# Six gate projections as seven half-size products each, and the neighbourhood query projection moved ahead

## The chip, the cores and the metric

One core of one Trainium2 chip runs the whole kernel in one launch. The metric is the device time of that launch in microseconds. All data are 32-bit floats.

## The reference, cut to what matters

One layer of a hybrid backbone for 256 latent tokens with 256 context tokens, 1024 wide. The normalised and modulated tokens `h` go through one wide input projection. Its parts feed a neighbourhood attention (nq, nk, nv), a gated scan in two directions (hq, ff, fb, hi, hg), a grouped-query attention (gq, gkv), and three gates of 1024 columns. Then the branches are merged and a mixture of 16 experts follows:

```python
zl = split_in(h_lat @ w_in)
zc = split_in(h_ctx @ w_in)
...
y_lat = branch_merge((a_lat, b_lat, c_lat), zl[11:14], w_branch, w_out)
...
def branch_merge(branches, gate_logits, w_branch, w_out):
    y = 0
    for i in range(N_BRANCHES):
        y = y + jax.nn.sigmoid(gate_logits[i]) * (branches[i] @ w_branch[i])
    return y @ w_out
```

The gates (`zl[11:14]`) are needed for the 256 latent tokens only; hi, nk and nv are needed for latent and context tokens alike.

## The kernel before

Five engines work side by side, each through an instruction list of its own, joined by semaphores. The order of each list is written out by hand; nothing is scheduled by a planner. TensorE (`pe`) multiplies, VectorE (`dve`) and ScalarE (`act`) empty its banks, GpSimd (`pool`) does side work, SyncE (`sp`) issues the transfers one after the other. A wait of any engine holds all that stands behind it in its list.

**Weights.** `FRONT` (line 43) lists the projections in the order of loading. Each takes a slot of 2 MB, three slots in turn (`SLOT_OF`); the load of a projection waits until the one three places ahead of it is multiplied (SP's loop, lines 486 to 527). Behind the loads of hq, hg, hi, nk, nq and nv, SP issues four each of 32 parts of the ada weights (`PARTS_BEHIND`, line 113), each as soon as GpSimd has used the part two before it (line 519); two more stand behind gq and six behind gate0. On the way to gate5 SP loads the first expert units, and one more (`load_unit(LAP - 3)`, line 499) when all pooled sums are done; `x_nat` is loaded behind gate2 (line 527).

**GpSimd's list.** After four sums of `hT` it goes through the parts q = 0 to 31 (line 620): a part of two 512-wide slices is multiplied by the conditioning (line 644 in one product of 1024 elements, or for q = 11 to 19 line 642 in two scalings of 512), and added into a running sum (lines 647 to 650). Between parts stand the operand sums for the projections that are computed in seven products: `weight_sums` (three sums of 128 x 1024, lines 606 to 609) and `last_weight_sum` (one, line 616), for hi before q = 9 and 12, for nk before q = 14 and 16, for nv before q = 20 and 24. Then come the rotary steps of the grouped-query attention (lines 660 to 678), ended by `gqa_ready`.

**Seven products.** hi, nk and nv (`SEVEN`, line 72) are 1024 x 512 weights times 1024 x 512 tokens. Each is cut in half in all three dimensions and computed as seven half-size products (`part_product`, line 937; 16 matmul records of 256 columns and 128 x 128 weights each, two records for one 32-bit matmul) in place of eight. Product 1 is copied out by ScalarE (`copy_first`), seven adds of VectorE (`add_product`, line 1671) combine them. Products 5 to 7 need operand sums of GpSimd, and product 3 needs the last one.

**The level stretch of TensorE** (lines 1195 to 1232). After the fills (`fill`, line 887) of ff, fb, hq, hg come eight levels of the scan, `level(0)` to `level(7)`. Each needs VectorE's `join` and ScalarE's `level_keys` of the level before. Between two levels lie two products of hi or nk. Behind level 7 stand both nq fills with the context state (`ctx_state`, line 1043) between them, then `across` (line 1022), the products of nv and the outputs.

**The attention loop** (line 1237) has 16 steps of eight heads and two tiles, neighbourhood attention first, then grouped-query. A step of TensorE is: scores (line 1113), in steps 0 to 5 one turn of a pooled sum, values of the step before (line 1136), one fill of gq, gkv or a gate, transposes of the normalised probabilities (line 1121). VectorE takes maxima, normalises (two scalings of 512, line 1791) and copies the transposes (line 1619); ScalarE takes exponentials. With steps 3 and 4 VectorE also squares and norms the grouped queries (line 1762). The 12 gate fills (line 908, 32 records of 256 columns) lie in steps 4 to 15; ScalarE copies them out. In step 7 the grouped queries and keys are turned, which needs `gqa_ready`. Behind the loop the branch projections br0 to br2 (line 925) begin at once.

## Time and profile before

| | us |
|---|---|
| median of 3 runs | 698.49 (697.67 to 698.77) |
| profiled execution | 697.12 |
| its span in the trace | 695.1 |
| TensorE busy (granted clock 0.997 on average) | 679.4 |
| VectorE, ScalarE, GpSimd busy | 325.3, 106.7, 239.1 |
| front stage up to the first products of hi | 0 to 116 |
| level stretch, up to the last product of nv | 116 to 231 |
| attention loop | 232 to 400 |
| branches, output projection, router | 400 to 483 |
| experts and end | 483 to 695 |

In the trace, a line names an engine, the line of the kernel, the operation, what it writes and reads, and a count. The busy time of TensorE is the union of its matmuls; they overlap in the pipeline, so that one lasts longer than it adds to a run of many. "Idle before" names the time an engine stood still ahead of a group, and what released it.

### The profile page before, as it was taken

To read this page: it belongs to the slowest core of one execution; us is meant where nothing else is said; L and a number is where in the kernel's file an instruction comes from. 1 tells how busy PE (TensorE), PEld (TensorE's weight loads), DVE (VectorE), ACT (ScalarE), POOL (GpSimd) and SP (SyncE) were. 2 spreads that over 40 slices of the span, in tenths; PEclk is the share of its full clock that TensorE was granted. 3 is DMA by queue.
4 is the path that set the end of the run, shared out by engine and by line. 5 is a ranking of instruction groups with operands and counts; after the bars stand their busy time and mean duration, and the time that the engine had idled before them with its cause. 6 is when DMAs were issued, how large, how long until landed. Compare 5 with 4: busy or idle time off the path is not lost.

```text
span 695.1 us, 8395 instructions
## 1 busy us (share of the span) xinstructions
PE 679.4 (98%) x3432; PEld 445.6 (64%) x3432; DVE 325.3 (47%) x531; ACT 106.7 (15%) x188; POOL 239.1 (34%) x155
## 2 busy tenths in 40 slices
PE   9999999999999999999999999999999999999995
PEld 5444587979989567777877888667435534434431
DVE  3459697796632687754343233336303203202214
ACT  4011011111001222321221140013000000000013
POOL 0029999999999594800000000000000000000014
PEclk9999999999999999999999999999999999999998
DMA  8993551341417744433491149866999999999993
GB/s 353 416 407 101 211 227 74 140 180 61 185 59 270 305 128 172 186 122 121 180 410 60 78 134 424 350 256 237 397 417 423 418 422 421 420 421 421 421 414 132
DMA packets 29512, 183.74 MB, mean 264 GB/s; under 512 B 3543, under 2 KB 5975, under 8 KB 14624
## 3 DMA queue, kind: packets, MB, share of 16 engines
q1 hardware_dynamic: 27456, 178.72, 64.7%
q0 software_dynamic: 1584, 3.97, 1.5%
q8 instruction: 29, 0.48, 0.3%
q10 hardware_dynamic: 432, 0.49, 0.2%
q14 instruction: 11, 0.09, 0.0%
HBM read 178.15 MB, written 6.82 MB: 266 GB/s over the span
## 4 chain that ended last, share of the span: by engine, by line
PE 75%; POOL 15%; DMA 4%; DVE 3%; issue 2%; ACT 1%; SPq 0%; POOLq 0%; DVEq 0%
PE bank L1431 21%; PE bank L908 14%; PE bank L944 6%; PE bank L925 6%; PE bank L1389 4%; POOL sb L644 3%; PE bank L931 3%; PE bank L1190 3%; PE bank L1113 2%; POOL sb L650 2%; PE bank L1136 2%; POOL sb L649 2%; PE bank L912 2%; PE bank L1121 2%; POOL sb L642 2%
## 5 line engine op out<-in xcount | busy, mean ns | idle before, releaser
L1431 PE MATMUL bank<-sb 128*64 128x512 f32 x768 | 166.8, 594 | 0.7 <-ACT sb L837 0.7
L685 POOL DMA_INDIRECT y_rows<-sb,token_rows x7 | 7.0, 1002 | 359.9 <-DVE sb L2049 335.1
L908 PE MATMUL bank<-sb 128*128 128x256 f32 x576 | 128.1, 381 | 0.0
L1431 PEld LDWEIGHTS bank<-sb 128*64 128x64 f32 x768 | 54.3, 137 | 106.5 <-issue 103.7
L908 PEld LDWEIGHTS bank<-sb 128*128 128x128 f32 x576 | 108.4, 190 | 16.2 <-issue 2.4
L944 PE MATMUL bank<-sb 128*128 128x256 f32 x336 | 74.1, 380 | 1.6 <-POOL sb L609 1.6
L944 PEld LDWEIGHTS bank<-sb 128*128 128x128 f32 x336 | 63.3, 190 | 9.9 <-POOL sb L609 1.8
L1619 DVE COPY sb<-bank 128x512 f32<-128x512 f32 x45 | 29.2, 684 | 82.5 <-PE bank L1121 54.4
L2009 DVE TENSOR_TENSOR sb<-sb,bank 128x512 f32<-128x512 f32 x8 | 5.5, 688 | 99.0 <-PE bank L1431 99.0
L644 POOL TENSOR_TENSOR sb<-sb 128x1024 f32<-128x1024 f32 x23 | 47.8, 2076 | 9.5 <-DMA sb<-ada_w 7.7
L925 PE MATMUL bank<-sb 128*128 128x256 f32 x192 | 41.9, 380 | 0.0
L925 PEld LDWEIGHTS bank<-sb 128*128 128x128 f32 x192 | 36.4, 190 | 5.0 <-issue 0.2
L650 POOL TENSOR_TENSOR sb<-sb 128x512 f32<-128x512 f32 x24 | 34.8, 1449 | 1.9
L642 POOL TENSOR_SCALAR sb<-sb 128x512 f32<-128x512 f32 x18 | 34.8, 1944 | 0.6
L649 POOL TENSOR_TENSOR sb<-sb 128x512 f32<-128x512 f32 x24 | 32.0, 1332 | 1.9
L2000 DVE TENSOR_SCALAR sb<-bank,sb 128x128 f32<-128x128 f32 x64 | 21.8, 404 | 17.8 <-PE bank L1389 17.6
L1190 PE MATMUL bank<-sb 128*128 128x512 f32 x64 | 29.0, 599 | 0.7 <-DVE sb L1571 0.7
L1389 PE MATMUL bank<-sb 128*128 128x128 f32 x224 | 27.9, 278 | 0.0
L904 PE MATMUL bank<-sb 128*128 128x512 f32 x64 | 27.6, 592 | 0.0
L792 ACT ACTIVATE sb<-bank,sb 128x512 f32<-128x512 f32 x32 | 21.8, 685 | 37.1 <-DVE sb L1784 37.1
L1389 PEld LDWEIGHTS bank<-sb 128*128 128x128 f32 x224 | 26.1, 192 | 0.0
L2049 DVE SCALAR_TENSOR_TENSOR sb<-bank,sb 128x512 f32<-128x512 f32 x14 | 10.5, 751 | 26.9 <-PE bank L1431 26.9
(260 smaller groups left out, 810.8 us busy)
## 6 DMA issues: line engine op xcount, KB each, us to landing
sb<-expert_w SPq DMA_DIRECT2D x90, 1024.0 KB, 17.6
sb<-front_w SPq DMA_DIRECT2D x19, 2048.0 KB, 8.4
sb<-ada_w SPq DMA_DIRECT2D x32, 512.0 KB, 3.7
sb<-ada_mix SPq DMA_DIRECT2D x4, 2048.0 KB, 19.8
sb<-expert_w SPq DMA_DIRECT2D x12, 512.0 KB, 10.9
sb<-xcT SPq DMA_DIRECT2D x4, 512.0 KB, 6.4
sb<-front_w SPq DMA_DIRECT2D x4, 512.0 KB, 20.5
y_rows<-sb SPq DMA_DIRECT2D x4, 512.0 KB, 24.0
```

Source lines behind the costliest of these rows:

```text
L642: last = pool.tensor_scalar(w[:, k, :], w[:, k, :], cvec[:, k0 + k, 0:1], None, ALU.mult)
L644: last = pool.tensor_tensor(w, w, cvec[:, k0:k0 + PART_K, 0:1].broadcast_to([P, PART_K, 512]), ALU.mult)
L649: link(pool.tensor_tensor(w[:, 0, :], w[:, 0, :], w[:, 1, :], ALU.add))
L650: ins = pool.tensor_tensor(ada_sum[g], ada_sum[g], w[:, 0, :], ALU.add)
L904: ins = pe.matmul(ps[:, :], lhs(w, k, i * P), hT[:, k, :], start=(k == 0), stop=(k == KD - 1))
L908: ins = pe.matmul(ps[:, c * L:(c + 1) * L], lhs(w, k, (2 * i + c) * P), hT[:, k, 0:L], start=(k == 0), stop=(k == KD - 1))
L925: ins = pe.matmul(ps[:, c * L:(c + 1) * L], lhs(w, k, (2 * i + c) * P, D), src[:, k, :], start=(k == 0), stop=(k == 3))
L944: ins = pe.matmul(o, left, right, start=(k == 0), stop=(k == 3))
L1190: ins = pe.matmul(banks[BANK_OF[i]][:, :], lhs(slot[0], k, i * P), hT[:, k, :], start=(k == 0), stop=(k == KD - 1))
L1389: ins = pe.matmul(banks[i][:, c * P:(c + 1) * P], x_nat[:, t, (4 * i + c) * P:(4 * i + c + 1) * P], S[:, t, :], start=(t == 0), stop=(t == ...
L1431: ins = pe.matmul(bank[e * CAP:(e + 1) * CAP, :], lhsT[:, k, e * CAP:(e + 1) * CAP], weights_at(k, e), start=(k == 0), stop=(k == parts - 1))
L1619: dve.tensor_copy(dst, shared_wait(n)[:, :]).then_inc(shared_out, 1)
```

## The change

Six things are changed. (1) The gates join `SEVEN`: each is cut in half in rows and columns of the weights and in tokens, so that its seven products are 128 columns wide (56 matmuls, 112 records). Products 2, 4 and 1 (`gate_first_half`) and 6, 7, 5 and 3 (`gate_second_half`) take the places of the two fills. GpSimd adds four sums per gate and four half-width sums of `hT` before q = 28; ScalarE copies product 1, VectorE adds seven products per gate. (2) nq is loaded ahead of hi, and its fills stand behind levels 0 and 1; the products of hi and nk move back by two levels, and the context state stands among those of nk. (3) GpSimd's sums for hi, nk and nv stand before later parts (13 and 16, 18 and 21, 24 and 26), and the two-scaling form is used from q = 5. (4) The sums of gate0 stand ahead of the rotary steps and those of the others behind them. (5) br0 waits until the last gate is summed. (6) `x_nat` and the expert unit LAP - 3 are loaded behind br2's weights. The diff, without bookkeeping of semaphore numbers, the renaming of waits and the rewritten `add_product`:

```diff
 ROUTES = GCOLS + NE
-FRONT = ["ff", "fb", "hq", "hg", "hi", "nk", "nq", "nv", "gq", "gkv"]
+FRONT = ["ff", "fb", "hq", "hg", "nq", "hi", "nk", "nv", "gq", "gkv"]
 FRONT += [f"gate{i}" for i in range(6)]
...
 WARM = (7, 4, 1, 3)
-BANK_OF = [{("ff", 3): 7, ("nq", 0): 0, ("nq", 1): 2}.get(f[:2], n % PBANKS) for n, f in enumerate(FILLS)]
+BANK_OF = [7 if f[:2] == ("ff", 3) else n % PBANKS for n, f in enumerate(FILLS)]
 ROW_GROUPS = (4, 5, 10, 11)
...
 PART_K = KD // PARTS
-PARTS_BEHIND = {name: range(4 * i, 4 * i + 4) for i, name in enumerate(("hq", "hg", "hi", "nk", "nq", "nv"))}
+PARTS_BEHIND = {name: range(4 * i, 4 * i + 4) for i, name in enumerate(("hq", "hg", "nq", "hi", "nk", "nv"))}
 PARTS_BEHIND["gq"], PARTS_BEHIND["gate0"] = range(24, 26), range(26, 32)
...
 STEPS = len(UNITS)
-FILLER = [n for n in range(fill_no("gq"), fill_no("br0"))]
+FILLER = [n for n in range(fill_no("gq"), fill_no("gate0"))]
 FILLER_AT = {i: [] for i in range(STEPS)}
 for _i, _n in enumerate(FILLER):
-    FILLER_AT[_i * STEPS // len(FILLER)].append(_n)
+    FILLER_AT[_i].append(_n)
 G_STEP = [i for i in range(STEPS) if fill_no("gkv", 1) in FILLER_AT[i]][0]
-GATE_FILLS = fill_no("gate5", 1)
+GATE_FILLS = fill_no("gate5")
+def gate_at(i):
+    return GATES[(i - len(FILLER)) // 2], (i - len(FILLER)) % 2
...
         w_sums = {"hi": [at(A0 + 1024 * i, 4, L) for i in range(2)]}
+        x_half_sums = [at(F0 + 8192 + 2048 + 512 * i, 4, P) for i in range(4)]
         w_sums["nk"] = w_sums["nv"] = [at(F0 + 2048 + 1024 * i, 4, L) for i in range(2)]
...
         spare = keep(NT * D, NT, D)
+        for g in GATES:
+            w_sums[g] = [spare[:, i, :].rearrange("p (k f) -> p k f", f=256) for i in range(2)]
         xT = [[at(C0 + 6144, 4, P), at(C0 + 6656, 4, P)],
...
         def out_part(name, fh, th):
+            if name in GATES:
+                c = 4 * GATES.index(name) + 2 * fh
+                return gates[:, c:c + 2, P * th:P * th + P]
             if name == "nk":
...
             return (v_hg if name == "hi" else na_v)[:, 2 * th:2 * th + 2, 256 * fh:256 * fh + 256]
-        def product_bank(name, m):
-            if m in part_bank:
-                return part_bank[m]
-            return banks[(m == 4) != (name != "hi")]
+        def x_half(kh, th):
+            return hT[:, 4 * kh:4 * kh + 4, P * th:P * th + P]
+        def product_out(name, m):
+            if name in GATES:
+                b, h = {1: (0, 0), 5: (0, 1), 3: (0, 0), 2: (1, 0), 4: (1, 1), 6: (2, 0), 7: (2, 1)}[m]
+                ps = banks[b][:, L * h:L * h + L]
+            else:
+                ps = (part_bank[m] if m in part_bank else banks[(m == 4) != (name != "hi")])[:, :]
+            return ps.rearrange("p (a b) -> p a b", a=2)
         def ada_place(g):
...
                     load_unit(8)
-                    sp.wait_ge(ada_summed, len(POOLED))
-                    load_unit(LAP - 3)
                 if name == "out0":
...
                     sp.dma_start(row5.rearrange("p (a b) -> p a b", a=2), d["b_rows"][:, 2:4, :]).then_inc(row5_in, 16)
+                if name == "br2":
                     sp.dma_start(x_nat, d["x_nat"]).then_inc(xnat_in, 16)
+                    load_unit(LAP - 3)
             sp.wait_ge(out_by["dve"], 4)
...
                     pool.wait_ge(fill_ready, multiplied("nk"))
+                if name in GATES[1:]:
+                    pool.wait_ge(part_ready, product_no(SEVEN[SEVEN.index(name) - 1], 5))
                 pool.tensor_tensor(s[0], w_part(name, 1, 0), w_part(name, 1, 1), ALU.add).then_inc(sums_ready, 1)
...
             def last_weight_sum(name):
-                pool.wait_ge(part_ready, product_no(name, 3))
+                pool.wait_ge(part_ready, product_no(name, 2))
                 pool.wait_ge(sums_ready, operand_no(name, 3))
...
             for q in range(PARTS * len(POOLED)):
-                if q == 9:
+                if q == 13:
                     weight_sums("hi")
-                if q == 12:
+                if q == 16:
                     last_weight_sum("hi")
-                if q == 14:
+                if q == 18:
                     weight_sums("nk")
-                if q == 16:
+                if q == 21:
                     last_weight_sum("nk")
-                if q == 20:
+                if q == 24:
                     weight_sums("nv")
-                if q == 24:
+                if q == 26:
                     last_weight_sum("nv")
+                if q == 28:
+                    pool.wait_ge(shared_out, shared_no("o", 1) + 1)
+                    link(pool.tensor_tensor(x_half_sums[0], x_half(0, 1), x_half(0, 0), ALU.subtract))
+                    link(pool.tensor_tensor(x_half_sums[1], x_half(1, 1), x_half_sums[0], ALU.subtract))
+                    pool.tensor_tensor(x_half_sums[2], x_half(1, 0), x_half_sums[1], ALU.subtract)
+                    pool.tensor_tensor(x_half_sums[3], x_half(1, 1), x_half(0, 1), ALU.subtract).then_inc(sums_ready, 1)
                 g, k0 = POOLED[q // PARTS], q % PARTS * PART_K
...
                 w = ada_part[q % 2].rearrange("p (k c) -> p k c", k=PART_K)
-                if 11 <= q < 20:
+                if 5 <= q < 20:
                     for k in range(PART_K):
...
                     pool.sem_inc(ada_summed, 1)
+            weight_sums(GATES[0])
+            last_weight_sum(GATES[0])
             pool.wait_ge(g_tab, 1)
...
             pool.tensor_tensor(kx, kx, gk, ALU.mult).then_inc(gqa_ready, 1)
+            for name in GATES[1:]:
+                weight_sums(name)
+                last_weight_sum(name)
             pool.wait_ge(rows_cleared, 16 * 2 * NT)
...
                     fill(n)
+                if i >= len(FILLER) and gate_at(i)[1] == 0:
+                    copy_first(gate_at(i)[0])
                 if i == G_STEP:
...
                     act.activation(g_ms, g_ms, ACT.Sqrt, bias=sm("eps"), scale=1.0 / HD).then_inc(rooted, 1)
-            act.wait_ge(out_by["act"], emptied(GATE_FILLS)[1])
+            act.wait_ge(out_by["sums"], emptied(GATE_FILLS)[1])
             for b in range(3):
...
                     wait_emptied(pe, before[-1])
-                if name == "nq":
-                    pe.wait_ge(out_by["sums"], sums_no("nk", 4))
                 if name == "gq":
                     wait_emptied(pe, fill_no("nv"))
+                if (name, i) == ("br0", 0):
+                    wait_emptied(pe, GATE_FILLS)
                 g = FRONT.index(name)
...
+            def gate_first_half(name):
+                g = GATES.index(name)
+                take_slot(FRONT.index(name))
+                if g == 0:
+                    wait_emptied(pe, fill_no("gkv", 1))
+                else:
+                    pe.wait_ge(out_by["sums"], sums_no(name, 0) - 3)
+                part_product(name, 2, w_part(name, 0, 1), x_half(1, 0))
+                pe.wait_ge(sums_ready, operand_no(name, 0))
+                part_product(name, 4, w_part(name, 1, 1), x_half_sums[2])
+                pe.wait_ge(out_by["sums"], sums_no(name, 0))
+                part_product(name, 1, w_part(name, 0, 0), x_half(0, 0))
+            def gate_second_half(name):
+                pe.wait_ge(sums_ready, operand_no(name, 2))
+                part_product(name, 6, w_sums[name][1], x_half_sums[1])
+                pe.wait_ge(sums_ready, operand_no(name, 3))
+                part_product(name, 7, w_part(name, 1, 0), x_half_sums[3])
+                pe.wait_ge(part_copied, SEVEN.index(name) + 1)
+                part_product(name, 5, w_sums[name][0], x_half_sums[0])
+                pe.wait_ge(sums_ready, operand_no(name, 4))
+                part_product(name, 3, w_part(name, 0, 1), x_half(1, 1))
             def take_shared(n):
...
             level(0)
+            fill(fill_no("nq", 0))
+            level(1)
+            fill(fill_no("nq", 1))
+            level(2)
             first("hi")
             fourth("hi")
-            level(1)
+            level(3)
             second("hi")
             sixth("hi")
-            level(2)
+            level(4)
             seventh("hi")
             fifth("hi")
-            level(3)
+            level(5)
             third("hi")
             first("nk")
-            level(4)
+            level(6)
             fourth("nk")
             second("nk")
-            level(5)
+            level(7)
             sixth("nk")
             seventh("nk")
-            level(6)
+            ctx_state()
             fifth("nk")
             third("nk")
-            level(7)
-            fill(fill_no("nq", 0))
-            ctx_state()
-            fill(fill_no("nq", 1))
             across()
...
                     fill(n)
+                if i >= len(FILLER):
+                    name, half = gate_at(i)
+                    (gate_first_half, gate_second_half)[half](name)
                 if i == GQA_TURN:
...
                 join(v)
-                if v == 2:
+                if v == 4:
                     sums_of_first("hi")
                     sums_of_seventh("hi")
-                if v == 3:
+                if v == 5:
                     sums_of_fifth("hi")
                     sum_of_third("hi")
-                if v == 5:
-                    sums_of_first("nk")
-                if v == 6:
-                    sums_of_seventh("nk")
-                    sums_of_fifth("nk")
-                if v == LEVELS - 1:
-                    sum_of_third("nk")
+            sums_of_first("nk")
+            sums_of_seventh("nk")
             for q in range(2):
                 shared_copy(shared_no("s0", q), S0[:, 4 * q:4 * q + 4, :].rearrange("p a b -> p (a b)"))
+            sums_of_fifth("nk")
+            sum_of_third("nk")
             for dr in range(2):
...
                     add_ada(g)
+                if i >= len(FILLER) and gate_at(i)[1] == 1:
+                    sums_of_first(gate_at(i)[0])
+                    sums_of_seventh(gate_at(i)[0])
                 if i == GQA_TURN:
...
                     shared_copy(shared_no("pT", 2 * i + e), probsT[:, e, :])
+                if i >= len(FILLER) and gate_at(i)[1] == 1:
+                    sums_of_fifth(gate_at(i)[0])
+                    sum_of_third(gate_at(i)[0])
                 if i == G_STEP:
```

## Rows read from the trace of the kernel before

**Rows 1.** The page: busy us; GB/s in 40 slices of 17.4 us

```profile
PE 679.4 (98%) x3432; PEld 445.6 (64%) x3432; DVE 325.3 (47%) x531; ACT 106.7 (15%) x188; POOL 239.1 (34%) x155
...
GB/s 353 416 407 101 211 227 74 140 180 61 185 59 270 305 128 172 186 122 121 180 410 60 78 134 424 350 256 237 397 417 423 418 422 421 420 421 421 421 414 132
```

**Rows 2.** Groups of instructions by line: busy us, mean ns of one, idle

```profile
L644 POOL TENSOR_TENSOR sb<-sb 128x1024 f32<-128x1024 f32 x23 | 47.8, 2076 | 9.5 <-DMA sb<-ada_w 7.7 <-POOL sb L650 0.5
...
L642 POOL TENSOR_SCALAR sb<-sb 128x512 f32<-128x512 f32 x18 | 34.8, 1944 | 0.6
...
L1389 PE MATMUL bank<-sb 128*128 128x128 f32 x224 | 27.9, 278 | 0.0
...
L1680 DVE TENSOR_TENSOR sb<-bank,sb 128x512 f32<-128x512 f32 x21 | 14.5, 689 | 9.9 <-PE bank L944 8.7
```

**Rows 3.** TensorE's timeline, level stretch: start, us, line, count, idle

```profile
154.05 7.15 PE L944 MATMUL bank<-sb 128*128 128x256 f32 x32 [1.62 <-POOL sb L609]
...
171.51 7.07 PE L944 MATMUL bank<-sb 128*128 128x256 f32 x32
178.42 1.95 PE L1011 MATMUL bank<-sb 128*128 128x128 f32 x16
180.21 7.07 PE L908 MATMUL bank<-sb 128*128 128x256 f32 x32
187.12 3.73 PE L1043 MATMUL bank<-sb 128*128 128x128 f32 x32
...
197.60 1.95 PE L1022 MATMUL bank<-sb 128*128 128x128 f32 x16
```

**Rows 4.** GpSimd in order of time, parts and operand sums

```profile
80.18 1.89 POOL L644 TENSOR_TENSOR sb<-sb 128x1024 f32<-128x1024 f32 x1
...
168.26 2.35 POOL L616 TENSOR_TENSOR sb<-sb 128x1024 f32<-128x1024 f32 x1 [0.24 <-POOL sb L650]
170.59 3.10 POOL L642 TENSOR_SCALAR sb<-sb 128x512 f32<-128x512 f32 x2
...
195.75 2.35 POOL L606 TENSOR_TENSOR sb<-sb 128x1024 f32<-128x1024 f32 x1 [0.24 <-POOL sb L650]
...
203.78 2.88 POOL L644 TENSOR_TENSOR sb<-sb 128x1024 f32<-128x1024 f32 x1
...
208.09 1.90 POOL L644 TENSOR_TENSOR sb<-sb 128x1024 f32<-128x1024 f32 x1
...
280.32 1.90 POOL L662 TENSOR_TENSOR sb<-sb 128x1024 f32<-128x1024 f32 x1 [11.44 <-DVE sb L1770]
```

**Rows 5.** TensorE in order of time, loop steps 4 and 15

```profile
277.88 7.17 PE L908 MATMUL bank<-sb 128*128 128x256 f32 x32
284.89 1.20 PE L1121 MATMUL bank<-sb 128*128 128x128 f32 x8
...
398.90 1.04 PE L1121 MATMUL bank<-sb 128*128 128x128 f32 x8
399.77 3.62 PE L925 MATMUL bank<-sb 128*128 128x256 f32 x16
```

**Rows 6.** VectorE in order of time, in the attention loop

```profile
256.94 3.06 DVE L1791 TENSOR_SCALAR sb<-sb 128x512 f32<-128x512 f32 x2
...
283.35 1.37 DVE L1791 TENSOR_SCALAR sb<-sb 128x512 f32<-128x512 f32 x2
...
329.00 1.29 DVE L1619 COPY sb<-bank 128x512 f32<-128x512 f32 x2 [4.75 <-PE bank L1121]
...
332.83 0.88 DVE L1791 TENSOR_SCALAR sb<-sb 128x512 f32<-128x512 f32 x2
339.08 1.29 DVE L1619 COPY sb<-bank 128x512 f32<-128x512 f32 x2 [5.38 <-PE bank L1121]
```

**Rows 7.** Busy time by stretch: each engine, PEclk, DMA share, GB/s

```profile
686.00:695.00 9.00, 1.61 (x4) 0.38 (x2) 3.88 (x7) 4.57 (x13) 2.52 (x3) 0.79 0.33 120
```

**Rows 8.** TensorE in order of time, its first work

```profile
1.33 5.16 PE L1164 MATMUL bank<-sb 128*128 128x256 f32 x14 [1.33 <-DVE sb L1532]
```

More of the change, by code:

```diff
@@ L66, in earlier, with product_no @@
     return [m for m in range(n) if SLOT_OF[m] == SLOT_OF[n]]
-SEVEN = ("hi", "nk", "nv")
+GATES = tuple(f"gate{i}" for i in range(6))
+SEVEN = ("hi", "nk", "nv") + GATES
 PRODUCTS = 6
-def product_no(name, last):
-    return PRODUCTS * SEVEN.index(name) + last
+def product_no(name, m):
+    return PRODUCTS * SEVEN.index(name) + ((2, 4, 1, 6, 7, 5) if name in GATES else (1, 4, 2, 6, 7, 5)).index(m) + 1
 def sums_no(name, last):
@@ L86, in operand_no @@
 def operand_no(name, last):
-    return 1 + 4 * SEVEN.index(name) + last
+    return 1 + (name in GATES) + 4 * SEVEN.index(name) + last
 def group_fills(name):
@@ L744, in fill @@
                     act.activation(gkv[:, 2 * i:2 * i + 2, :], two, ACT.Copy).then_inc(done, 1)
-                elif name[:4] == "gate":
-                    c = 4 * int(name[4:]) + 2 * i
-                    if c == 0:
-                        act.wait_ge(shared_out, shared_no("s0", 1) + 1)
-                    act.activation(gates[:, c:c + 2, :], two, ACT.Copy).then_inc(done, 1)
             def level_keys(v):
@@ L762, in copy_first @@
                     act.wait_ge(silu_hg, 2)
-                act.activation(out_part(name, 0, 0), product_bank(name, 1)[:, :].rearrange("p (a b) -> p a b", a=2),
-                               ACT.Copy).then_inc(part_copied, 1)
-            for n in range(fill_no("hi")):
+                act.activation(out_part(name, 0, 0), product_out(name, 1), ACT.Copy).then_inc(part_copied, 1)
+            for n in range(fill_no("nq")):
                 fill(n)
```

45 lines of the change are left out of this document (22 added, 23 removed).

## Prediction

> **What bounds the kernel now.** First the busy shares: TensorE is busy for 98% of the span, VectorE 47%, GpSimd 34% [rows 1]. So any TensorE time that is removed comes off the end, unless something else becomes late. Then TensorE's order of time in the level stretch [rows 3]: the reader is to see one stream without holes except 1.62 us in front of a product, and its releaser, the GpSimd line L609. So GpSimd is nearly late there already. Its own timeline [rows 4] shows it working without a pause from 80 to 222 us: it is the second engine of this stage, and its 34% is an average over a span in whose second half it idles. Last the attention loop: TensorE has its 7.0 us fill in every step and the softmax chain of VectorE and ScalarE lies beside it [rows 5, 6].
>
> **The change part by part.**
>
> *Gate products.* How far apart do records follow each other? A run of 32 with 256 columns lasts 7.07 us and the next line starts 6.91 after its start, so 0.216 us each; a run of 32 with 128 columns, each with a weight block of its own, lasts 3.73 us, of which the last record's length is 0.278: (3.73 - 0.278) / 31 = 0.111 us [rows 2, 3]. A gate is now two fills of 32 records; one takes 7.01 us from its start to that of the transposes behind it (277.88 to 284.89) [rows 5], 0.1 more than 32 x 0.216. After: 7 products x 8 matmuls x 2 records = 112 records x 0.111 = 12.5, plus twice 0.1, 12.7 us against 14.0. Six gates: -8.0 us, all on TensorE, which sets the end. Range of the pitch: 0.111 to 0.1245 (the group of L1389 over its count, 27.9/224) [rows 2], so between -8.0 and +0.5. I take 0.111, as the row is a like stream.
>
> The Trainium skill ("TensorE: Matmul & The Clock Gate", "Back-to-back issue gap") speaks against this edit: it says that in a stream of weight load and matmul pairs the spacing is set by both, and gives 81 ns where the columns alone would take 56. By its ratio 1.45 the 112 records would take about 18.1 us and the gates would get slower, by some 24 us in all. The trace disagrees: half the columns come at 52% of the pitch [rows 3].
>
> *GpSimd's queue before attention.* This is the costly part. `last_weight_sum("nk")` stood before part q = 16 of the pooled ada sums; it now stands before q = 21, and TensorE's product 3 of nk waits for it. GpSimd is a serial queue: it ends that sum at 168.26 + 2.35 = 170.6 us now [rows 4]. Ahead of it come q = 16 to 19 (170.59 to about 195.5, 24.9 us), q = 20 (203.78 to 208.09, 4.3, of which 1.0 is contention that will then lie later: 3.3) [rows 4], and six parts q = 5 to 10 change from one 1.89 us product to two scalings of together 3.10 us [rows 4], 1.2 each, 7.2 in all. Sum 170.6 + 24.9 + 3.3 + 7.2 = 206.0 us. When will TensorE want it? Third product of nk now starts at 171.51 + 3.53 = 175.0. Ahead of it are now put level 7 (1.8), both nq fills (6.9 each) and the context state (3.6) [rows 3]: 19.2 us, and the 1.6 us wait goes: 192.6. So TensorE waits 13.4 us there, and `across` starts at 206.0 + 3.45 = 209.4 instead of 197.60 [rows 3]: +11.8 us. An earlier wait, on the last sum of hi, is paid within this one. Bounds: the conversion may cost up to 1.8 us a part (twice the mean of L642 less that of L644) [rows 2], +3.6; or less contention of VectorE in 97 to 112 us and in the levels may give up to 6 back. So +6 to +16.
>
> Moving nq ahead costs TensorE nothing in itself: same records, its weights simply take the turn of hi's. The weights of hi now follow parts 8 to 11 in SP's queue, so they are asked for when q = 9 is done, about 113 us, and are wanted at 134 by TensorE and about 131 by GpSimd; cover of some 9 us after a load. The nv sums: GpSimd from 206 takes q = 21 to 23 (14 us) and three sums of 2.35 (the first at 195.75 now) [rows 4], more if VectorE contends, to about 229; TensorE wants the third of them 11.8 us later than now, at about 232. Cover 3 us, cost nothing; if it is gone, the same amount late.
>
> *Clock.* TensorE would stand still for over 8 us, which it does nowhere between its first and last work now. The only such row: at the end, TensorE stops at 687.6 and the mean granted clock of 686 to 695 is 0.79 [rows 7], thus the lower level, 1.2 GHz, for about 3.8 us. And from the first standstill: 14 records in 5.16 us [rows 8] where 13 x 0.216 + 0.38 = 3.2 would do. So 0 to 2 us; I take 1.5.
>
> *Step 4 of the loop.* The fill of step 4 ends just when the normalised rows are ready: the transposes at 284.89 carry a stretch of 1.20 us instead of 1.04, and VectorE ends the scaling at 283.35 + 1.37 = 284.7 [rows 5, 6]. The first half of gate0 takes 48 x 0.111 + 0.1 = 5.5 instead of 7.0, so 1.5 of the gain cannot be had here. Besides, GpSimd, now idle from 268.9 to 280.3 [rows 4] (its q = 26 must wait for a transfer behind gate0's weights, before and after), will then do the four half sums of hT (4 x 1.3) and the rest of the pooled parts, and gate0's sums fall on VectorE's squares (L1762, two 1024-element operands) and scaling. Two 0.44 us scalings took 3.06 us when they met GpSimd's work [rows 6]. So 1 to 4.6 us; I take 3.5. The Trainium skill ("GPSIMD Engine Reference", "Specifications") says the two engines share SBUF interfaces, in contention when VectorE has two SBUF inputs or a 2-port mode; the 3.06 us agrees.
>
> *Other steps.* VectorE adds seven sums per gate, 256 columns each; nearest rows 0.69 us for 512 [rows 2], so 0.35 to 0.69, taken as 0.45. Four lie while TensorE multiplies 5 and 3; three come after the copies of the turned probabilities and delay the next maxima by 1.4 us. From the copies' start to the end of the next scaling are 4.7 us now (329.00 to 333.71) in a step of 10.1 (329.00 to 339.08) [rows 6]; they become 6.1 in a step that with the short fill is 8.6 long, and the transposes want the scaling some 0.7 before the copies: cover 1.8 us. Cost nothing; if GpSimd's 2.35 us sum collides each time, up to 0.5 x 5. ScalarE's copy per gate replaces two. The rope work of GpSimd moves behind gate0's sums, to about 7 us before it is wanted at step 7 (16 us long, from 280.3 now).
>
> *End of the loop.* br0 now waits for gate5's last sum. Before, it starts at 399.77 directly behind the transposes of 398.90 [rows 5]. After: copies end 1.0 us behind the transposes, three sums 1.4: +2.5 us, with nothing for TensorE beside it (values of step 15 stand behind br0). Bounds 2 to 3.2.
>
> *Transfers.* x_nat and the 1 MB unit move behind br2's weights, about 400 us, where 78 to 134 GB/s are moved [rows 1]; both are wanted much later. Nothing; were they late, 2.4 us each.
>
> *Sum* against the profiled execution (697.12 us, span 695.1): +11.8 +1.5 -8.0 +3.5 +2.5 = +11.3, 708.4 us. The median of the runs is 1.4 us above the profiled one: **709.8 us**.
>
> **The rivals.**
> (a) *GpSimd is in time.* If contention rather than work makes its queue long, and it ends nk's last sum by 192.6, the wait goes and also the 1.6 us of now: -8.0 +2.5 +1 -1.6 = -6, 692.5 us. For it: GpSimd products stretch from 1.89 to 2.88 us [rows 4]. Against: this needs 13 us out of a queue in which five added parts alone are 28 us, at 6.2 us each for q = 16 to 19 [rows 4].
> (b) *It is a little late.* Ending at 195 to 201: total -2 to +4, 697 to 702.5.
> (c) *Weight loads bound the half products.* Were each record to wait for its own load (192 ns as L1389's) a gate takes 21.5 us: +45 instead of -8, about 762. It decides from 0.123 us a record on, where the gates gain nothing. Against: 0.111 in a like stream [rows 3]. The Trainium skill's ratio, above, would give about 742 instead.
> The forecast itself, a late last sum of nk, gives a loss for any end later than about 197.
>
> **How the numbers follow.** Forecast 0.70, its own range 703 to 715; (a) 0.15; (b) 0.11; (c) 0.04. The range 697 to 715 takes in the forecast and (b). A difference of 0.2% (1.4 us) is about what a measurement of this kernel tells from none. Faster: (a), 0.15. Within: about half of (b), 0.06. Slower: the rest, 0.79.
>
> **What would show it.** Right: TensorE idle some 8 to 13 us before nk's third product, released by GpSimd's L616 counterpart near 206; `across` near 209; 128-column records at 0.111; a step pair of about 18.8 us instead of 20.2; idle of 2.5 before br0; a step 4 no shorter than now. Wrong: no GpSimd releaser in the levels (then a), or records at over 0.12 (then c). My weakest number is the length of GpSimd's queue.

## The result

| | before | after |
|---|---|---|
| median, us | 698.56 (697.67 to 698.77, 4 runs) | 715.25 (712.19 to 715.85, 4 runs) |
| profiled execution | 697.12 | 714.96 |
| its span | 695.1 | 713.2 |
| TensorE's granted clock | 0.997 | 0.978 |

The ratio after over before is 1.0233, 95% interval 1.0202 to 1.0263: slower by 16.7 us at the median and by 18.1 us between the two spans. The forecast was 709.8 us in a range of 697 to 715; the measured median is 5.4 us above the forecast and 0.25 us above the upper end of the range; the ratio, taken of the 698.49 us known ahead of the prediction, gives 714.8 us, just inside it. Of two kernels below, e2_wide and e9_both, one run each (1179 and 1425 us) was disturbed and is left out of their medians.

The page of after, which answers to [rows 1] (busy us and share; PEclk in 40 slices of 17.8 us):

```profile
PE 681.4 (96%) x3720; PEld 453.8 (64%) x3720; DVE 348.7 (49%) x573; ACT 101.9 (14%) x182; POOL 308.9 (43%) x189
PEclk9999999997989999979999999999999999999999
PE 67%; POOL 22%; DVE 5%; DMA 3%; issue 2%; ACT 1%; POOLq 0%; DVEq 0%
```

TensorE is busy for 2.0 us more than before although it multiplies less, GpSimd has 70 us more, and the third line (the chain that ended last) gives GpSimd 22% of the span, where it was 15% before. The clock dips in the slices that begin at 160, 196 and 303 us: twice in the level stretch and once at step 4 of the loop. These are the two places where the time went.

**The level stretch.** TensorE's order of time, which answers to [rows 3]:

```profile
167.81 10.15 PE L973 MATMUL bank<-sb 128*128 128x256 f32 x32 [7.80 <-POOL sb L638]
...
205.58 6.59 PE L973 MATMUL bank<-sb 128*128 128x256 f32 x16 [3.20 <-POOL sb L638]
212.00 1.95 PE L1076 MATMUL bank<-sb 128*128 128x128 f32 x16
```

L638 is `last_weight_sum`. TensorE waits for it twice, 7.80 us for that of hi and 3.20 us for that of nk. The products behind the waits take 10.15 and 6.59 us where the same records took 7.07 and 3.62 [rows 3; the 16 records of nk as those of br0 in rows 5]. `across` (L1076) starts at 212.00 instead of 197.60, and the first scores of the loop at 246.92 instead of 232.51: +14.4 us.

The chain of after says the same from GpSimd's side (start, us, engine and line):

```profile
187.13 3.09 POOL sb L670 x2
...
203.18 2.35 POOL sb L638
205.53 0.04 issue
205.58 6.59 PE bank L973 x16
```

Between these lines the chain runs through the pooled parts on GpSimd alone, without a wait, and nk's last sum ends at 205.53. The prediction had 206.0.

**Step 4 of the loop.** TensorE in order of time:

```profile
303.27 1.11 PE L1175 MATMUL bank<-sb 128*128 128x128 f32 x4 [5.12 <-DVE sb L1844]
304.84 1.09 PE L1175 MATMUL bank<-sb 128*128 128x128 f32 x4 [0.46 <-DVE sb L1605]
305.86 2.08 PE L1167 MATMUL bank<-sb 64*128 64x512 f32 x4
307.87 2.08 PE L1154 MATMUL bank<-sb 128*128 128x512 f32 x2
...
311.14 7.41 PE L973 MATMUL bank<-sb 128*128 128x128 f32 x64
```

and the same place of before:

```profile
286.02 1.13 PE L1113 MATMUL bank<-sb 64*128 64x512 f32 x4
287.07 1.13 PE L1100 MATMUL bank<-sb 128*128 128x512 f32 x2
```

TensorE stands still for 5.12 and 0.46 us, and then the scores and the turn of a pooled sum take 2.08 us each instead of 1.13. Why VectorE is late, in its own order of time and in GpSimd's:

```profile
290.33 1.73 DVE L1815 TENSOR_TENSOR sb<-sb 128x1024 f32<-128x1024 f32 x1
291.98 2.83 DVE L1817 TENSOR_TENSOR sb<-sb 128x512 f32<-128x512 f32 x1
...
297.32 2.23 DVE L1823 TENSOR_SCALAR sb<-sb 128x16 f32<-128x16 f32 x1
```

```profile
288.62 2.36 POOL L628 TENSOR_TENSOR sb<-sb 128x1024 f32<-128x1024 f32 x1 [0.18 <-POOL sb L678]
291.06 3.21 POOL L630 TENSOR_TENSOR sb<-sb 128x1024 f32<-128x1024 f32 x1
294.23 2.81 POOL L631 TENSOR_TENSOR sb<-sb 128x1024 f32<-128x1024 f32 x1
```

The sums of gate0 (a fourth, L638, follows at 297.18) cover the squares (L1815, L1817) and even a scaling of 16 elements (L1823, 2.23 us). Both engines are stretched.

**The gates and br0** (TensorE, one gate at steps 8 and 9; the end of the loop; then the group of all gate records: count, busy us, mean ns, idle before):

```profile
342.19 5.62 PE L973 MATMUL bank<-sb 128*128 128x128 f32 x48
347.65 1.04 PE L1175 MATMUL bank<-sb 128*128 128x128 f32 x8
...
350.72 7.41 PE L973 MATMUL bank<-sb 128*128 128x128 f32 x64
357.97 1.04 PE L1175 MATMUL bank<-sb 128*128 128x128 f32 x8
...
418.18 3.69 PE L954 MATMUL bank<-sb 128*128 128x256 f32 x16 [2.61 <-DVE sb L1736]
...
L973 PE MATMUL bank<-sb 128*128 128x128 f32 x672 | 78.1, 277 | 0.0
```

From the start of a half to that of its transposes: 5.46 + 7.25 = 12.71 us a gate, against twice 7.01 [rows 5]. No record of a gate waits for anything. br0 waits 2.61 us for VectorE's last add.

**The account.** TensorE's starts of like work, after less before: `across` +14.4 (212.00 and 197.60), fill of step 5 +22.0 (311.14 and 289.15), br0 +18.4 (418.18 and 399.77), end of the span +18.1. Split up, with what slowed records take over their usual time counted as clock: levels without clock +11.4, clock +6.2 (nk's third product 3.0, step 4 3.2), gates 6 x -1.31 = -7.9, step 4 without clock +5.9, br0 +2.8, rest -0.3: +18.1.

### The profile page after: what moved, and what is told of

It is laid out like the page before. It is cut to its first block, busy times and chain, and to the rows that moved or that the text cites. A ratio compares the mean times of both kernels' runs of the same rounds, so it can differ in the third digit from the quotient of the medians.

```text
span 713.2 us, 9091 instructions
## 1 busy us (share of the span) xinstructions
PE 681.4 (96%) x3720; PEld 453.8 (64%) x3720; DVE 348.7 (49%) x573; ACT 101.9 (14%) x182; POOL 308.9 (43%) x189
## 4 chain that ended last, share of the span: by engine, by line
PE 67%; POOL 22%; DVE 5%; DMA 3%; issue 2%; ACT 1%; POOLq 0%; DVEq 0%
PE bank L1488 20%; PE bank L973 14%; POOL sb L670 8%; PE bank L954 6%; PE bank L1446 4%; POOL sb L678 3%; PE bank L960 3%; POOL sb L677 3%; PE bank L1244 3%; PE bank L1167 2%; PE bank L1190 2%; PE bank L941 2%; PE bank L1175 2%; POOL sb L672 2%; DMA sb<-y_rows 1%
## 5 line engine op out<-in xcount | busy, mean ns | idle before, releaser
L973 PE MATMUL bank<-sb 128*128 128x128 f32 (+1 forms) x1008 | 158.3, 318 | 11.0 <-POOL sb L638 11.0
L973 PEld LDWEIGHTS bank<-sb 128*128 128x128 f32 x1008 | 143.2, 195 | 23.3 <-POOL sb L638 11.6
L670 POOL TENSOR_SCALAR sb<-sb 128x512 f32<-128x512 f32 x30 | 56.7, 1899 | 1.4 <-POOL sb L678 0.4
L1736 DVE TENSOR_TENSOR sb<-bank,sb 128x256 f32<-128x256 f32 (+1 forms) x63 | 32.3, 512 | 42.4 <-PE bank L973 38.3
L954 PE MATMUL bank<-sb 128*128 128x256 f32 x192 | 41.9, 380 | 2.6 <-DVE sb L1736 2.6
L672 POOL TENSOR_TENSOR sb<-sb 128x1024 f32<-128x1024 f32 x17 | 35.0, 2058 | 16.7 <-DMA sb<-ada_w 15.6
L937 PE MATMUL bank<-sb 128*128 128x256 f32 x192 | 42.1, 379 | 0.0
L954 PEld LDWEIGHTS bank<-sb 128*128 128x128 f32 x192 | 36.3, 190 | 7.8 <-issue 3.0
L937 PEld LDWEIGHTS bank<-sb 128*128 128x128 f32 x192 | 36.3, 190 | 5.2 <-issue 0.5
L628 POOL TENSOR_TENSOR sb<-sb 128x1024 f32<-128x1024 f32 x9 | 22.2, 2467 | 39.1 <-PE bank L973 38.6
L1844 DVE TENSOR_SCALAR sb<-sb 128x512 f32<-128x512 f32 x32 | 29.5, 962 | 0.6
L1244 PE MATMUL bank<-sb 128*128 128x512 f32 x64 | 29.0, 599 | 0.7 <-DVE sb L1628 0.7
```

Of the source, the lines that this page charges most:

```text
L670: last = pool.tensor_scalar(w[:, k, :], w[:, k, :], cvec[:, k0 + k, 0:1], None, ALU.mult)
L672: last = pool.tensor_tensor(w, w, cvec[:, k0:k0 + PART_K, 0:1].broadcast_to([P, PART_K, 512]), ALU.mult)
L937: ins = pe.matmul(ps[:, c * L:(c + 1) * L], lhs(w, k, (2 * i + c) * P), hT[:, k, 0:L], start=(k == 0), stop=(k == KD - 1))
L954: ins = pe.matmul(ps[:, c * L:(c + 1) * L], lhs(w, k, (2 * i + c) * P, D), src[:, k, :], start=(k == 0), stop=(k == 3))
L973: ins = pe.matmul(o, left, right, start=(k == 0), stop=(k == 3))
L1244: ins = pe.matmul(banks[BANK_OF[i]][:, :], lhs(slot[0], k, i * P), hT[:, k, :], start=(k == 0), stop=(k == KD - 1))
```

## The experiments

All times are medians, with lowest and highest; the ratio is to the kernel before on the same chip, which took 697.35 us beside the first four kernels, 697.74 beside the next four and 697.44 beside the last, and 698.56 beside after. So kernels of different groups are compared by what they take over the kernel before: for after that is 16.7 us. The theory: a late GpSimd queue makes the level stretch, two engines in one another's way make step 4, and each standstill adds a low clock behind it. The rivals stand in each expectation.

**1. Put GpSimd's sums earlier** (e1_queue, an edit of after):

```diff
                 if q == 13:
                     weight_sums("hi")
-                if q == 16:
+                if q == 14:
                     last_weight_sum("hi")
-                if q == 18:
+                if q == 16:
                     weight_sums("nk")
-                if q == 21:
+                if q == 18:
                     last_weight_sum("nk")
-                if q == 24:
+                if q == 21:
                     weight_sums("nv")
-                if q == 26:
+                if q == 23:
                     last_weight_sum("nv")
```

> Only the places of GpSimd's operand sums in its queue change against the changed kernel: hi's last sum before q = 14 (was 16), nk's three sums before 16 (18) and its last before 18 (21), nv's before 21 and 23 (24 and 26). Theory A (the position in GpSimd's serial queue makes TensorE wait, and the wait drops TensorE's clock): both waits of 7.8 and 3.2 us and the two stretches at 1.2 GHz (3.1 and 3.0 us longer than normal) go, across starts near 195 instead of 212.0, the whole takes about 17 us less, some 698. Rival B (the level stretch is late because nq was moved and the parts were turned into two scalings, whatever the order): across stays above 205 and the whole above 708. Rival C (GpSimd's total work is too long, the order only moves the wait): nk's wait goes, but a wait of about as much appears at nv's products; across near 195, last nv product no earlier than 240.

Measured: 709.93 us (709.33 to 710.77), ratio 1.0175 [1.0158, 1.0192], span 709.0. TensorE, VectorE and the transfers' queue (SPq) in order of time:

```profile
192.83 5.41 PE L973 MATMUL bank<-sb 128*128 128x256 f32 x16 [1.90 <-POOL sb L638]
...
233.14 1.13 PE L1167 MATMUL bank<-sb 64*128 64x512 f32 x4
...
245.86 2.17 PE L1175 MATMUL bank<-sb 128*128 128x128 f32 x8 [4.13 <-DVE sb L1844]
```

```profile
242.05 0.43 DVE L1834 TENSOR_TENSOR bank<-bank,sb 128x256 f32<-128x256 f32 x1 [9.82 <-DMA sb<-na_bias]
```

```profile
225.15 7.30 SPq L540 DMA_DIRECT2D sb<-ada_w  x2
...
232.97 0.43 SPq L536 DMA_DIRECT2D sb<-na_bias  x1
```

The first scores start at 233.14, 13.8 us earlier than in after and 0.6 us later than before: the places of these sums in GpSimd's queue are the cause of the level stretch. But the kernel still takes 12.6 us over the kernel before, only 4.1 us less than after, where 698 us had been expected. The pooled parts that were pushed back by the sums hold SP: it issues the table `na_bias` at 232.97, behind two ada parts, VectorE waits 9.82 us for it in step 0, and TensorE 4.13 us, with slow records behind (eight transposes in 2.17 us instead of 1.04). The table was nearly late in the kernel before already: issued at 227.44, it held VectorE for 2.31 us there (start 233.91), without a wait of TensorE. Moving the operand sums forward in GpSimd's queue made what stood behind them late, and the late thing was a transfer that the code of GpSimd doesn't name.

**2. One product instead of two scalings for q = 5 to 10** (e2_wide: `if 11 <= q < 20` as before).

> Against the changed kernel only the form of the pooled products for q = 5 to 10 goes back to one product of 1024 elements (two scalings only from q = 11). Theory A: each part is 1.2 us shorter or more, so nk's last sum ends 7 to 8 us earlier, near 198; hi's last sum near 160.5, when TensorE wants it at 160.0; TensorE waits for nk's last sum some 3 to 5 us; across near 203 to 205, whole about 706 to 708. Rival (VectorE, meeting longer GpSimd instructions from 80 to 120 us, delays level 0 and the levels): level 0 starts 1 us or more later than 113.5 and across gains under 4 us.

Measured: 711.83 us (710.71 to 712.01, 3 runs), 1.0198 [1.0176, 1.0219]. nk's third product:

```profile
201.91 5.24 PE L973 MATMUL bank<-sb 128*128 128x256 f32 x16 [7.57 <-POOL sb L638]
```

It starts 3.7 us earlier than in after, where the sum has 7.2 for six parts, and `across` at 206.99 instead of 203 to 205. The wait on hi's last sum is 0.84 us instead of 7.80, but that on nk's has grown from 3.20 to 7.57. Level 0 starts at 113.72, 0.2 us later than in after, so the rival (VectorE delayed there) isn't the reason. Where did the rest go? GpSimd's first sum for hi starts at 126.27 in e2_wide and at 134.65 in after: up to there the conversion costs 8.4 us, as priced or more. At the last sum of hi the lead is 6.8 us (158.65 and 165.41), and at the first of nk 2.9 (175.31 and 178.16). Between these two stand the same two parts, 14.3 us long in e2_wide and 10.4 in after. Their first scalings, e2_wide and then after:

```profile
160.98 5.13 POOL L670 TENSOR_SCALAR sb<-sb 128x512 f32<-128x512 f32 x2
```

```profile
167.73 3.10 POOL L670 TENSOR_SCALAR sb<-sb 128x512 f32<-128x512 f32 x2
```

VectorE joins the same level in both, from 160.9 to 166.0 in e2_wide and from 160.7 to 166.6 in after. In e2_wide GpSimd's two scalings lie on that work, and the adds behind them (2.26 us at 170.75, 2.14 at 173.09, against 1.27 each in after) on the next join, and all are stretched. In after they come later, while VectorE stands still for 7.90 us (166.6 to 174.5) behind the late sum of hi, and run at their own speed. A standstill of the others gives GpSimd part of its delay back, and a shorter queue loses it again.

**3. Hold gate0's sums until the squares are done** (e3_hold: `pool.wait_ge(g_rec, 1)` ahead of `weight_sums(GATES[0])`).

> Against the changed kernel GpSimd waits with gate0's operand sums until VectorE has finished the norms of the grouped queries (step 4). Theory A (the stall of step 4 is made by GpSimd's gate0 sums meeting VectorE's squares and scalings, and the clock falls behind the stall): the wait ahead of step 4's transposes falls from 5.1 us to under 1.5, the clock stays up, VectorE's squares take 1.2 and 0.7 us instead of 1.7 and 2.8; whole about 7 to 8 us less, 707 to 708. Rival B (the stall is there because the fill is 1.5 us shorter and VectorE's chain is what it is): the wait stays above 3 us. Rival C (holding the sums makes gate0's second half wait in step 5): a new wait of 3 us or more on GpSimd in step 5, whole not below 712.

Measured: 714.91 us (711.25 to 716.07, 5 runs), 1.0248. No gain at the median, where 7 to 8 us had been expected. The profiled execution is the fastest of the five, and even there step 4 gets back only a part (TensorE, then VectorE):

```profile
298.14 0.66 PE L1176 MATMUL bank<-sb 128*128 128x128 f32 x4 [1.87 <-DVE sb L1845]
301.31 1.07 PE L1176 MATMUL bank<-sb 128*128 128x128 f32 x4 [2.52 <-DVE sb L1606]
```

```profile
288.45 1.22 DVE L1816 TENSOR_TENSOR sb<-sb 128x1024 f32<-128x1024 f32 x1
...
296.11 4.46 DVE L1845 TENSOR_SCALAR sb<-sb 128x512 f32<-128x512 f32 x2
```

The squares are back at 1.22 and 0.68 us (L1818, at 289.58), so they were slow for the overlap with GpSimd. But the sums now lie on the two scalings, which take 4.46 us instead of 1.37. The collision was moved, not removed. From the fill of step 4 to that of step 5 this execution takes 15.96 us, after 18.62 and the kernel before 11.27. Why the other four executions are no faster than after isn't shown; their mean clocks are 0.978 to 0.982 against 0.987 here.

**4. Keep TensorE at work in step 4** (e4_warm: eleven throw-away products ahead of step 4's transposes; the output is not touched).

```diff
+                if i == 4:
+                    for _ in range(11):
+                        pe.matmul(banks[2][:, 0:256], ident, small[:, 0:256], start=True, stop=True)
                 turn_probs(i)
```

> Against the changed kernel TensorE does 11 throw-away matmuls of 256 columns (22 records x 0.216 = 4.75 us) in step 4 between gate0's first half and the transposes, that is inside the stall of 5.1 us. Theory A (behind the stall 3.5 us are lost because the clock is at 1.2 GHz): the stall's end stays at about the same distance, the scores and the pooled turn of step 5 go back from 2.08 to 1.13 us each, the whole takes 3 to 3.5 us less, about 711.8. Rival (these operations are slow because VectorE or GpSimd hold the memory or the banks): they stay slow and the whole stays within 1 us of the changed kernel.

Measured: 711.84 us (709.89 to 713.78), 1.0214 [1.0193, 1.0235].

```profile
299.88 0.66 PE L1175 MATMUL bank<-sb 128*128 128x128 f32 x4 [0.37 <-DVE sb L1847]
301.46 0.63 PE L1175 MATMUL bank<-sb 128*128 128x128 f32 x4 [0.92 <-DVE sb L1608]
302.02 1.13 PE L1167 MATMUL bank<-sb 64*128 64x512 f32 x4
```

The kernel takes 14.5 us over the kernel before, 2.2 less than after; the two intervals overlap, so it is the trace that shows the gain. VectorE is no earlier: the transposes start 10.74 us behind the fill, 10.75 in after. The scores take 1.13 us again instead of 2.08, and the granted clock is 1.00 from 296 to 312 us. From fill to fill step 4 takes 16.02 us instead of 18.62, so work that nobody needs saves 2.6 us there. The 3.2 us counted above are the whole excess of the slowed records; about 0.5 of them lay inside the second wait for VectorE, which is 0.92 us here and 0.46 in after. VectorE's share of step 4 is then 6.5 us rather than 5.9. The rest of the lead of this execution comes from nk's third product, which isn't slowed in it (last section).

**5. Each half of the change alone.** e5_gates is after with the order of the projections, the forms of the parts and GpSimd's q positions of before, so only the gates and what goes with them (the wait of br0, `x_nat` and the expert unit behind br2) are changed; e6_nq is before with nq ahead, two scalings from q = 5 and the new positions, and each gate as two fills.

> The gates' half of the change alone: gates as seven products, with the level stretch, the nq fills and GpSimd's sums for hi, nk and nv in the order of the kernel before. Theory A (level stretch and gates add up; in the changed kernel the levels cost 14.4 us and the rest 3.7): scores of step 0 at 232.5 as before, stall of some 5 us at step 4's transposes, 2.6 us before br0, about 3.5 us over the kernel before: 701. Rival (the stall of step 4 and its lowered clock come only from the lateness that the level stretch hands on): no stall over 1.5 us, about 692 to 694.

> The other half alone: nq moved ahead, GpSimd's sums at q = 13, 16, 18, 21, 24, 26 and two scalings from q = 5, gates as two fills of 256 columns as before. Theory A: waits of about 7.8 and 3.2 us in the level stretch, each with a stretch at 1.2 GHz behind it, attention begins 14 us later than before, and nothing of it is won back: 711 to 712. Rival (the loop takes up the delay, as the loads and GpSimd's pooled sums are then in time): under 706.

Measured: e5_gates 703.31 us (701.38 to 703.76), 1.0079 [1.0063, 1.0096], +5.6; e6_nq 710.39 us (707.77 to 710.94), 1.0169 [1.0144, 1.0194], +12.7. The sum is +18.3 where after has +16.7, so the halves add up to within the spread of the runs. They come 2.3 and 0.6 us from what was expected (701, and 711 to 712), and both rivals fall: the stall of step 4 is there without the late level stretch, and the loop takes up nothing of the delay. Each has its own waits and not the other's (e5_gates, then e6_nq):

```profile
288.88 1.12 PE L1177 MATMUL bank<-sb 128*128 128x128 f32 x4 [5.12 <-DVE sb L1849]
```

```profile
167.48 9.99 PE L942 MATMUL bank<-sb 128*128 128x256 f32 x32 [7.80 <-POOL sb L616]
...
205.24 6.43 PE L942 MATMUL bank<-sb 128*128 128x256 f32 x16 [3.35 <-POOL sb L616]
```

Even the gates, which save 7.9 us of TensorE, are a loss alone.

**6. The gates alone, with gate0's sums early** (e7_early, an edit of e5_gates). GpSimd adds the half sums of hT and gate0's first three sums ahead of q = 26, in a gap in which it waited for that part, into a buffer of their own.

```diff
         for g in GATES:
             w_sums[g] = [spare[:, i, :].rearrange("p (k f) -> p k f", f=256) for i in range(2)]
+        w_sums[GATES[0]] = [at(F0 + 6144 + 1024 * i, 4, L) for i in range(2)]
...
-                if q == 28:
+                if q == 26:
                     pool.wait_ge(shared_out, shared_no("o", 1) + 1)
...
+                    weight_sums(GATES[0])
...
-            weight_sums(GATES[0])
             last_weight_sum(GATES[0])
```

> e5_gates with gate0's three operand sums and the half sums of hT moved ahead of part q = 26, into GpSimd's idle time in front of that part (7.7 us in the kernel before), with a buffer of their own. Theory A (the stall of step 4 is GpSimd's gate0 sums meeting VectorE's squares and norms): the stall falls to about 1 us, which the shorter fill leaves, the clock stays at 2.4 GHz, about 7 us less than e5_gates: 693 to 694. Rival (the stall is VectorE's chain itself, longer than the short fill): a stall of over 3 us remains, no better than 698.

Measured: 698.18 us (696.78 to 700.35, 10 runs), 1.0010 [0.9997, 1.0023]: 5.1 us less than e5_gates and still not faster than the kernel before, where 693 to 694 us had been expected.

```profile
285.73 0.66 PE L1178 MATMUL bank<-sb 128*128 128x128 f32 x4 [1.08 <-DVE sb L1850]
287.61 1.09 PE L1178 MATMUL bank<-sb 128*128 128x128 f32 x4 [1.22 <-DVE sb L1608]
...
400.58 5.19 PE L957 MATMUL bank<-sb 128*128 128x256 f32 x16 [2.60 <-DVE sb L1739]
```

Step 4's standstill falls from 5.58 to 2.30 us, of which the shorter fill by itself lays open 1.5. The low clock, which the expectation had gone, is still paid, at step 4 (scores of 2.08 us) and at br0 (5.19 us for what took 3.62).

**7. br0 without its wait** (e8_banks, an edit of e7_early). br0's first fill goes to bank 1, which the gate's fourth add frees; only the second fill waits for the last.

```diff
-BANK_OF = [{("ff", 3): 7, ("nq", 0): 0, ("nq", 1): 2}.get(f[:2], n % PBANKS) for n, f in enumerate(FILLS)]
+BANK_OF = [{("ff", 3): 7, ("nq", 0): 0, ("nq", 1): 2, ("br0", 0): 1, ("br0", 1): 0}.get(f[:2], n % PBANKS) for n, f in enumerate(FILLS)]
...
                 if (name, i) == ("br0", 0):
+                    pe.wait_ge(out_by["sums"], sums_no("gate5", 4))
+                if (name, i) == ("br0", 1):
                     wait_emptied(pe, GATE_FILLS)
```

> e7_early and the banks of br0's first two fills exchanged, so that the first goes to a bank that gate5 has left by its fourth sum. Theory A: the 2.6 us of idle before br0 go, 2.5 us less than e7_early, about 691, and this beats the kernel before by 6 us. Rival (the time is given back behind, since the sigmoids of the gates still wait for the last sum and VectorE's products for them): under 0.8 us gained.

Measured: 696.30 us (694.57 to 696.82, 10 runs), 0.9973 [0.9964, 0.9983]. No wait at br0 any more:

```profile
399.67 1.04 PE L1180 MATMUL bank<-sb 128*128 128x128 f32 x8
400.54 1.68 PE L959 MATMUL bank<-sb 128*128 128x256 f32 x7
```

1.9 us less than e7_early, where 2.5 had been expected; wait and clock together had been 4.2 there. The profiled execution is one of the two slowest of the ten (696.82 us) and has a low clock at level 0 (16 records in 3.45 us at 114.42) that the one of e7_early doesn't have (2.02 us at 114.35), although both stood still about equally long ahead of it (1.26 and 0.34 us, 1.31 and 0.34).

**8. Both remedies** (e9_both, an edit of e8_banks: three throw-away products ahead of each of step 4's two groups of transposes).

```diff
             def turn_probs(i):
                 for e in range(2):
+                    if i == 4:
+                        for _ in range(3):
+                            pe.matmul(banks[2][:, 0:256], ident, small[:, 0:256], start=True, stop=True)
                     pe.wait_ge(norm_ready, 2 * i + e + 1)
```

> Kernel e8_banks (half-size gates alone, early sums, swapped banks) with three throw-away products of 256 columns ahead of each of the two groups of transposes in step 4, where TensorE stood still for 1.09 and 1.22 us and then ran at 1.2 GHz from 289.3 to about 295 us. Clock theory: the standstill itself stays (VectorE's scaling and add still set the two starts, about 287.4 and 289.2), but TensorE keeps 2.4 GHz, so the scores behind it take about 1.1 us instead of 2.08 and the other records of 289 to 295 half as long: about 2.5 to 3 us less than e8, 693.5 us, ratio to the kernel before about 0.993 to 0.995. Rival (the low clock there costs nothing, since later waits set the pace): no change against e8, 696.3 us, ratio 0.997, and steps 5 to 15 would show waits that e8 does not have. Rival 2 (the throw-away products only add their own 1.3 us each, as they end later than the wait): 697 to 698 us.

Measured: 694.49 us (694.46 to 697.19, 5 runs), 0.9956 [0.9943, 0.9969], 2.95 us less than the kernel before beside it. The two kernels' fills of step 5, e8_banks and then e9_both:

```profile
295.97 7.41 PE L978 MATMUL bank<-sb 128*128 128x128 f32 x64
```

```profile
289.95 1.13 PE L1172 MATMUL bank<-sb 64*128 64x512 f32 x4
...
293.09 1.16 PE L978 MATMUL bank<-sb 128*128 128x128 f32 x8
...
311.23 0.66 PE L1183 MATMUL bank<-sb 128*128 128x128 f32 x4 [1.75 <-DVE sb L1855]
```

The fill starts 2.9 us earlier, as expected. The medians give 1.8 of them, or 1.5 when each is set against the kernel before beside it. The profiled execution was the slowest of the five (697.19 us) and has a new wait of 1.75 us in step 6, where GpSimd's sums for gate1 now meet VectorE's two scalings (4.27 us). Whether the others, 694.46 to 694.99 us long, have it is open, and the intervals of e8_banks and e9_both overlap a little.

## Why the prediction came out right, and where it was short

- **GpSimd's queue in the level stretch: right.** Its end was put at 206.0 us and came at 205.5; the forecast of the start of `across` was 209.4, and 212.0 was measured, the difference being the clock. That the end was met to 0.5 us is in part luck, as two terms are off in opposite directions: e2_wide shows the conversion at 8.4 us where it was priced at 7.2, and the parts q = 16 to 19 take 23.1 us in after (167.73 to 178.16 and 187.11 to 199.8) where 24.9 was taken over. Of the 8.4 us only 3.7 reach TensorE when they are taken away, since the contention changes with the queue. The place of the wait was wrong: 13.4 us were put before nk's third product, and TensorE stands still 3.20 there and 7.80 before hi's. The prediction had that wait as "paid within this one", and so it is, with the 3.1 us of low clock behind it: nk's product can't start before 205.5 either way.
- **Clock: the mechanism right, the size wrong.** The term was 1.5 us, at most 2, from one standstill. In after the slowed records cost 3.0 us at nk's third product and 3.2 in step 4 (2.6 by e4_warm), 6.2 us together. The prediction had counted only the long standstill in the levels, though its own term for step 4 contained another. This is the largest miss, +4.7 by the account (+4.1 with e4_warm's figure).
- **Gates: right.** Forecast -8.0, measured -7.9; 12.71 us a gate where the pitch of 0.111 us gives 12.6, and no record waits, so rival (c) falls. The ratio that the prediction weighed from the Trainium skill ("TensorE: Matmul & The Clock Gate", "Back-to-back issue gap"), 81 ns where the columns alone would take 56, isn't seen in this trace: records of 128 columns follow each other at 0.113 us (7.25 us for 64), 52% of the 0.216 us of those of 256.
- **Step 4: the right place and cause, the wrong size.** Taken as 3.5, within 1 to 4.6; the account has 5.9 without the clock and e4_warm 6.5, above the upper end. The 1.5 us of the short fill were right; the term that was too small is the collision, left with 2.0 us and measured at 4.7. Its bound came from one row in which two scalings met GpSimd's work, but four sums in a row met three instructions of VectorE: 1.73 for 1.22, 2.83 for 0.68 and 2.23 for 0.17, together 4.7 us. The Trainium skill ("GPSIMD Engine Reference", "Specifications") puts the contention at instructions of VectorE with two SBUF inputs or in a 2-port mode; the squares, which have two such inputs, agree. Whether the slow L1823 (a scaling of 16 elements, 2.23 us) falls under it, no run here shows.
- **br0: right**, 2.5 against 2.6 to 2.8. The low clock behind it in e5_gates and e7_early (5.38 and 5.19 instead of 3.62) wasn't in after's profiled execution (3.69).
- **Costs set to nothing:** the rotary steps, the loads of hi's weights, x_nat and the expert unit show no wait in after. In the other steps of the loop there are only the waits of the kernel before, 1.13 us in step 3 (0.89 before) and 0.44 in step 7 (0.44 before).
- **Rivals (a) and (b)** needed GpSimd to end nk's sum by 192.6 or by 201. In e1_queue, which has it at 192.8, the level stretch's loss is gone as (b) says, but (b) hadn't seen that the parts behind it carry a transfer that step 0 needs.

e7_early gained 5.1 us at the median and its trace 3.0 us (spans of 696.6 and 699.6): the profiled execution of e5_gates, 701.38 us, lies 1.9 below its median. What stays open: how often each of the short standstills is followed by the low clock, and why four of five executions of e3_hold gained nothing.

## What to carry to other kernels

Saved TensorE time counts only where the helpers' work moves with it: before a projection gets operand sums, write out the helper's serial queue with its due times, and the transfers that wait for its parts as well. The same products gave +5.6 us with the sums where they fit the code and -1.4 us with gate0's sums in an idle gap and the bank freed earlier, and -2.95 us with TensorE kept at work besides. Where two engines stretch one another, look for a gap, since a later place only moves the collision; and price each new standstill of TensorE at its own length plus the slow records behind it, up to 3 us each here.

## What the runs showed of the hardware

- A standstill of 5.1 us, and even two of 1.1 and 1.2 us close together (e7_early, e8_banks), was followed by records at 1.2 GHz (granted clock 0.50 in after), which cost 2.6 us in after, 1.5 in e7_early and 3.0 in e8_banks. Waits of 1.13 us (step 3 of after) and 1.62 us (the kernel before, [rows 3]) were not followed by it. After's windows (start and end; PE, PEld, DVE, ACT and POOL busy; PEclk; DMA share; GB/s) behind the first:

```profile
303.30:306.00 2.70, 2.24 (x10) 1.54 (x10) 2.62 (x5) 0.00 (x0) 2.62 (x3) 0.50 0.00 0
...
308.00:311.00 3.00, 3.00 (x18) 1.46 (x18) 2.12 (x4) 1.56 (x4) 2.84 (x4) 0.60 0.00 0
311.00:315.00 4.00, 4.00 (x38) 3.87 (x35) 1.90 (x4) 0.00 (x1) 3.53 (x9) 1.00 0.00 0
```

- It isn't the same in each execution: nk's third product came in 6.59 us in after behind 3.20 us of waiting, but in 3.72 in e4_warm behind 3.44, and in 5.24 in e2_wide behind 7.57, so the loss doesn't follow the length of the wait. The time of an execution goes with its mean clock: the five of e7_early at 0.998 took 696.78 to 697.94 us, the five at 0.990 to 0.997 took 698.42 to 700.35. That would explain why kernels with standstills spread over up to 5 us while the kernel before spreads over 1 to 2; no run tested it by itself.
- Transposes follow the clock as well (four in 1.11 us at 303.27, in 0.66 in e4_warm), and throw-away products in a standstill keep it up.
- Contention runs both ways and isn't in proportion: two scalings took 0.88 us alone and up to 4.46 beside GpSimd's sums, a sum 2.35 alone and up to 3.37.
